# Gate and up of a SwiGLU feed-forward with the weights held in the array: 80 of 88 blocks computed transposed, in a two-layer-type transformer on one core

## The reference

```python
D_MODEL, SEQ, D_FF = 1024, 256, 2816

def rms_norm(x, g):
    y = x * lax.rsqrt(jnp.mean(x * x, axis=-1, keepdims=True) + 1e-6)
    return y * g

def swiglu(x, w_gate, w_up, w_down):
    return (jax.nn.silu(x @ w_gate) * (x @ w_up)) @ w_down

h = h + 0.5 * swiglu(rms_norm(h, g), w_gate, w_up, w_down)   # eight times, mixers between them
```

## Time and profile before

| | |
|---|---|
| median of 3 runs | 1973.38 us |
| lowest, highest | 1972.54, 1973.45 us |
| profiled execution, first to last instruction (the only time that it has) | 1971.0 us |
| PE, PEld busy | 1960.5, 1652.8 us |
| DVE, ACT, POOL busy | 1199.4, 1018.6, 68.9 us |
| TensorE clock granted | 1.000 |
| share of PE in the chain that ended last | 95% |

### The profile page before, as it was taken

The page is one execution under the profiler, slowest core; times in us unless marked ns, Lnnn a source line. Parts: engine busy times, 40 slices in busy tenths (PEclk is TensorE's granted clock), DMA queues, the critical chain, the costliest instruction groups (busy, mean ns, idle before and its releaser), DMA issues.

```text
span 1971.0 us, 26229 instructions
## 1 busy us (share of the span) xinstructions
PE 1960.5 (99%) x9838; PEld 1652.8 (84%) x9838; DVE 1199.4 (61%) x1817; ACT 1018.6 (52%) x1590; POOL 68.9 (3%) x77
## 2 busy tenths in 40 slices
PE   9999999999999999999999999999999999999999
PEld 7888988888888898888888898888888888888887
DVE  6555656556655566555755566655576555876554
ACT  6444555445554665444544447544475444755442
POOL 0100300000000000000000000000010000200000
PEclk9999999999999999999999999999999999999999
DMA  9655436553655426555555434555446553306550
GB/s 339 210 202 174 150 108 214 192 191 130 221 184 178 144 77 212 192 192 171 188 181 186 162 138 139 203 192 192 171 163 234 183 189 128 108 24 212 192 192 22
DMA packets 241050, 338.91 MB, mean 172 GB/s; under 512 B 5728, under 2 KB 206351, under 8 KB 240831
## 3 DMA queue, kind: packets, MB, share of 16 engines
q1 hardware_dynamic: 239710, 335.84, 50.5%
q0 software_dynamic: 496, 1.23, 0.2%
q10 hardware_dynamic: 752, 0.61, 0.1%
HBM read 336.61 MB, written 1.05 MB: 171 GB/s over the span
## 4 chain that ended last, share of the span: by engine, by line
PE 95%; DVE 2%; ACT 2%; DMA 1%; issue 0%; SPq 0%; POOL 0%; ACTq 0%
PE A L535 11%; PE A L537 11%; PE A L536 11%; PE G L535 10%; PE G L537 10%; PE G L536 10%; PE X L535 8%; PE X L537 8%; PE X L536 8%; PE A L1226 1%; PE A L904 1%; PE G L964 1%; PE X L964 1%; PE X L1210 1%; PE G L1238 1%; DVE wl L496 0%
## 5 line engine op out<-in xcount | busy, mean ns | idle before, releaser
L496 DVE TENSOR_TENSOR wl<-raw,wh 128x1024 fp32r<-128x1024 f32 (+1 forms) x553 | 653.8, 1221 | 121.3 <-ACT wh L487 120.3
L487 ACT ACTIVATE wh<-raw 128x1024 fp32r<-128x1024 f32 (+1 forms) x553 | 561.9, 1058 | 144.1 <-PE A L537 102.6
L535 PE MATMUL G<-wh,xh 128*128 128x512 f32 (+1 forms) x814 | 322.1, 396 | 0.2
L537 PE MATMUL G<-wh,xl 128*128 128x512 f32 (+1 forms) x814 | 317.2, 390 | 0.0
L536 PE MATMUL G<-wl,xh 128*128 128x512 f32 (+1 forms) x814 | 316.3, 389 | 0.0
L535 PE MATMUL X<-wh,xh 128*128 128x512 f32 x672 | 265.8, 395 | 0.3 <-DVE wl L496 0.3
L537 PE MATMUL X<-wh,xl 128*128 128x512 f32 x672 | 262.3, 390 | 0.0
L536 PE MATMUL X<-wl,xh 128*128 128x512 f32 x672 | 261.6, 389 | 0.0
L537 PEld LDWEIGHTS G<-wh,xl 128*128 128x128 f32 x814 | 152.8, 188 | 32.3
L535 PEld LDWEIGHTS G<-wh,xh 128*128 128x128 f32 x814 | 152.9, 188 | 30.9 <-DVE xl L2399 0.6
L536 PEld LDWEIGHTS G<-wl,xh 128*128 128x128 f32 x814 | 153.1, 188 | 29.9
(11 more groups left out here) (487 smaller groups left out, 2787.5 us busy)
## 6 DMA issues: line engine op xcount, KB each, us to landing
raw<-in_ffn_w_in SPq DMA_DIRECT2D x88, 1024.0 KB, 6.8
raw<-in_ffn_w_down SPq DMA_DIRECT2D x44, 1024.0 KB, 6.5
raw<-in_ffn_w_out SPq DMA_DIRECT2D x44, 1024.0 KB, 7.1
raw<-in_ffn_w_gate SPq DMA_DIRECT2D x42, 1024.0 KB, 5.5
raw<-in_ffn_w_up SPq DMA_DIRECT2D x42, 1024.0 KB, 7.5
raw<-in_a_w_in SPq DMA_DIRECT2D x12, 1024.0 KB, 6.1
raw<-in_ab_w_in SPq DMA_DIRECT2D x8, 1024.0 KB, 6.8
raw<-in_kv_w SPq DMA_DIRECT2D x6, 1024.0 KB, 6.5
```

Source lines behind the costliest of these rows:

```text
L487: nc.scalar.activation(hi, r, ACT.Copy).then_inc(hi_done[u], 1)
L496: nc.vector.tensor_tensor(lo, r, hi.bitcast(F32), ALU.subtract).then_inc(lo_done[u], 1)
L535: nc.tensor.matmul(o, sh, rh, start=start, stop=False)
L537: return nc.tensor.matmul(o, sl, rh, start=False, stop=stop)
```

## The change

In blocks 1 to 10 of every feed-forward the weights of gate and of up are stationary, 128 hidden columns at a time, and the tokens move. `xh` and `xl` are put side by side in one buffer `xs`, so one matmul of 512 columns gives high weights by high tokens (first half of the bank) and high weights by low tokens (second half). Eight of these and eight matmuls of 256 columns (low weights by high tokens, into the first half) make one bank: 128 hidden columns of gate or of up. A half of a block is now 128 hidden columns with all 8 chunks of channels. The hidden block comes out with hidden columns on partitions, so it isn't transposed.

The two halves of a bank are added by ACT (`lows`, copies the second half to SBUF) and DVE (`sums`). The factor of a token now runs along the free axis. DVE multiplies gate by `tok_rstd` (`normed`), ACT takes Silu (`gate`), DVE multiplies by up (`hidden`), ACT and DVE split (`hid_hi`, `hid_lo`). The factor of up is left to the residual add, which multiplies by `half_rstd` in place of 0.5. Block 0 stays as it was in its matmuls and is transposed, into banks A, with Silu in place of Sigmoid. Each feed-forward makes `tok_rstd` once by `turn_factor` with a matrix of ones. In ffn0 the loads of block 1 are cut by columns (512 bytes in a row in place of 1024).

The diff, cut to its core:

```diff
-        xh = sb("xh", [P, KC, S], F32R)
-        xl = sb("xl", [P, KC, S], F32R)
+        xs = sb("xs", [P, 2, KC, S], F32R)
+        xh, xl = xs[:, 0, :, :], xs[:, 1, :, :]
...
+            if spec == "ffn" and u < 2 and block not in first_ffn_blocks:
+                mode, shape = "cols", (KC, P)
+            elif spec == "ffn":
...
                     for u, w in ((0, gate), (1, up)):
-                        load_rows(sp, w, 1, u, slice(0, 4), raw_landed[1][u])
+                        load_cols(w, 1, u, 0, raw_landed[1][u])
...
                     tile = base + 2 * b + half
+                    if b > 1:
+                        pe.wait_ge(sums_done, 20 * f + 2 * (b - 2) + half + 1 + at)
+                    for u in (0, 1):
+                        pe.wait_ge(lo_done[u], n_of[tile, u] + at)
+                        _, sh, sl = half_views(tile, u)
+                        bank = GB[1 - half][u]
+                        for c in range(KC):
+                            mm(bank[:, :].rearrange("p (a s) -> p a s", a=2), sh[:, c, :], xs[:, :, c, :], start=c == 0,
+                               stop=False)
+                        for c in range(KC):
+                            last = mm(bank[:, 0:S], sl[:, c, :], xh[:, c, :], start=False, stop=c == KC - 1)
+                    last.then_inc(used[1], 1)
...
                 def step(b, turn=None):
                     gate_up(b, 0, turn)
-                    turn_hid(b - 1, turn)
+                    if b == 1:
+                        turn_first_hid()
+                        turn_factor(name, tok_rstd_in, ones)
                     gate_up(b, 1, turn)
                     down(b - 1, turn)
...
                 gate_up(end, 0)
-                turn_hid(end - 1)
                 gate_up(end, 1)
                 wait_down(end - 1)
...
-                    if q == 3:
-                        turn_hid(end)
...
-            def turn_factor(k):
+            def turn_factor(name, src, every):
-                pe.wait_ge(event("factor_in"), k)
+                pe.wait_ge(event("factor_in"), FACTOR[name])
                 for t in range(NT):
-                    last = mm(A[2][:, t * P:(t + 1) * P], tri[:, P:S], factor_in[:, t, :], start=True, stop=True)
+                    last = mm(A[2][:, t * P:(t + 1) * P], every, src[:, t, :], start=True, stop=True)
...
+                def lows(b, half, turn=None):
                     at = 0 if turn is None else 4 * turn
+                    by, n = done_at[base + 2 * b + half, 1]
                     act.wait_ge(used[by], n + at)
-                        A_(sig[:, t, :], GB[b % 2][t][:, 0:S], ACT.Sigmoid, scale=rstd[:, t:t + 1]).then_inc(sig_ready, 1)
+                    for u, dst in ((0, gate_n), (1, up_n)):
+                        last = A_(dst[:, half, :], GB[1 - half][u][:, S:2 * S], ACT.Copy)
+                    last.then_inc(low_out, 1)
...
+                def step(b, turn=None):
+                    for half in (0, 1):
+                        for u in (0, 1):
+                            prepare_hi(base + 2 * b + half, u, turn)
+                        lows(b - 1, half, turn)
+                    gate(b - 1, 0, 2, turn)
                     for half in (0, 1):
                         prepare_hi(base + 2 * b + half, 2, turn)
-                    hid_hi(b - 1, turn)
+                    hid_hi(b - 1, 0, 2, turn)
...
+                end = FFN_BLOCKS - 1
+                lows(end, 0)
                 prep(name, FT, (0, 1))
-                sigmoid(FFN_BLOCKS - 1)
+                gate(end, 0, 1)
+                hid_hi(end, 0, 1)
+                lows(end, 1)
+                gate(end, 1, 1)
...
+                def sums(b, half, turn=None):
                     at = 0 if turn is None else 4 * turn
+                    dve.wait_ge(low_out, 20 * f + 2 * (b - 1) + half + 1 + at)
+                    for u, dst in ((0, gate_n), (1, up_n)):
+                        last = V.tensor_tensor(dst[:, half, :], GB[1 - half][u][:, 0:S], dst[:, half, :], ALU.add)
+                    last.then_inc(sums_done, 1)
...
+                def step(b, turn=None):
+                    for half in (0, 1):
+                        for u in (0, 1):
+                            prepare_lo(base + 2 * b + half, u, turn)
+                        sums(b - 1, half, turn)
+                    normed(b - 1, 0, 2, turn)
+                    prepare_lo(base + 2 * b, 2, turn)
+                    hidden(b - 1, 0, 2, turn)
+                    prepare_lo(base + 2 * b + 1, 2, turn)
+                    hid_lo(b - 1, 0, 2, turn)
```

More of the change, by code:

```diff
@@ L931, in gate_up @@
                                 pe.wait_ge(lo_done[u], PIECE_AT[tile][i])
-                        if b == 0 and (tile or i):
+                        if tile or i:
                             if half == 0 and i == 2:
@@ L1787, in ffn, with first_gate, first_hid_hi @@
                 f, base = int(name[3:]), T0[name]
-                def sigmoid(b, turn=None):
+                def first_gate():
+                    by, n = done_at[base + 1, 1]
+                    act.wait_ge(used[by], n)
+                    for t in range(NT):
+                        A_(silu[:, t, :], GB[0][t][:, 0:S], ACT.Silu, scale=rstd[:, t:t + 1]).then_inc(silu_ready, 1)
+                def first_hid_hi():
+                    for t in range(NT):
+                        act.wait_ge(hid_turned, 2 * f + t + 1)
+                        A_(hidh[:, 0, t * S:(t + 1) * S], A[t][:, 0:S], ACT.Copy).then_inc(hidh_done, 1)
@@ L1797, in hid_hi, with gate @@
+                def gate(b, first, n, turn=None):
                     at = 0 if turn is None else 4 * turn
[L1798 to L1802, removed]
+                    act.wait_ge(gate_ready, 20 * f + 2 * (b - 1) + first + n + at)
+                    A_(silu[:, first:first + n, :], gate_n[:, first:first + n, :], ACT.Silu).then_inc(silu_ready, n)
@@ L1935, in fox_mixer @@
                 start("fox")
-                factor_out(1)
+                factor_out("fox")
                 def split_keys(b):
@@ L2457, in hid_lo, with first_hidden @@
-                def hid_lo(b, turn=None):
-                    at = 0 if turn is None else 4 * turn
-                    for t in range(NT):
-                        dve.wait_ge(hidh_done, 2 * (FFN_BLOCKS * f + b) + t + 1 + at)
-                        part = slice(t * S, (t + 1) * S)
-                        V.tensor_tensor(hidl[:, b % 2, part], GB[b % 2][t][:, 0:S], hidh[:, b % 2, part].bitcast(F32),
-                                        ALU.subtract).then_inc(hidl_done, 1)
-                def step(b, turn=None, split=(), downs=()):
+                def first_hidden():
+                    for t in range(NT):
+                        dve.wait_ge(silu_ready, 2 * FFN_BLOCKS * f + t + 1)
+                        V.tensor_tensor(hid[:, t, :], GB[0][t][:, S:2 * S], silu[:, t, :], ALU.mult).then_inc(hid_done, 1)
@@ new lines, in first_hid_lo @@
+                def first_hid_lo():
+                    for t in range(NT):
+                        dve.wait_ge(hidh_done, 2 * FFN_BLOCKS * f + t + 1)
+                        part = slice(t * S, (t + 1) * S)
+                        V.tensor_tensor(hidl[:, 0, part], A[t][:, 0:S], hidh[:, 0, part].bitcast(F32), ALU.subtract
+                                        ).then_inc(hidl_done, 1)
+                def sums(b, half, turn=None):
+                    at = 0 if turn is None else 4 * turn
+                    dve.wait_ge(low_out, 20 * f + 2 * (b - 1) + half + 1 + at)
+                    for u, dst in ((0, gate_n), (1, up_n)):
+                        last = V.tensor_tensor(dst[:, half, :], GB[1 - half][u][:, 0:S], dst[:, half, :], ALU.add)
+                    last.then_inc(sums_done, 1)
@@ new lines, in normed, with hidden @@
+                def normed(b, first, n, turn=None):
+                    at = 0 if turn is None else 4 * turn
+                    dve.wait_ge(sums_done, 20 * f + 2 * (b - 1) + first + n + at)
+                    part = gate_n[:, first:first + n, :]
+                    V.tensor_tensor(part, part, wide(tok_rstd.unsqueeze(1), n, S), ALU.mult).then_inc(gate_ready, n)
+                def hidden(b, first, n, turn=None):
+                    at = 0 if turn is None else 4 * turn
+                    dve.wait_ge(silu_ready, 2 * (FFN_BLOCKS * f + b) + first + n + at)
+                    part = slice(first, first + n)
+                    V.tensor_tensor(hid[:, part, :], up_n[:, part, :], silu[:, part, :], ALU.mult).then_inc(hid_done, n)
@@ L2466, in step, with hid_lo, first_step @@
+                def hid_lo(b, first, n, turn=None):
+                    at = 0 if turn is None else 4 * turn
+                    dve.wait_ge(hidh_done, 2 * (FFN_BLOCKS * f + b) + first + n + at)
+                    to, hi = (x[:, b % 2, S * first:S * (first + n)].rearrange("p (j s) -> p j s", s=S) for x in (hidl, hidh))
```

(2 more changed lines are left out.)

153 lines of the change are left out of this document (85 added, 68 removed).

## The result

The changed kernel takes 1959.13 us (median of four runs, 1959.00 to 1959.45) against 1973.04 us for the kernel before in the same comparison (1972.54 to 1973.45). The ratio is 0.9931, with a 95% interval of 0.9919 to 0.9943. The prediction was 1958.8 us, in a range of 1955 to 1966: 14.6 us less than the 1973.38 of the three runs before it, where 13.9 were measured.

What follows compares the result with a forecast made beforehand. PE was taken to bound the kernel, busy 1960.5 of 1971.0 us. 1971.0 - 18.3 (blocks) + 3.7 (factor) = 1956.4 us, with 2.4 us from span to median 1958.8 us; range 1955 to 1966 us.

Steps and rivals of the forecast that it cites:

- Transposes: PE, blocks 1 to 10: four transposes removed at 0.443 us a block, -35.4 us; 0.05 a block left as a rest.
- Gate and up: PE, blocks 1 to 10: 16 more matmuls a block cost +0.213 us each block, +17.1 us in all.
- changing between the widths costs nothing: PE, gate and up: going between matmuls of 512 and 256 columns adds no time, 0.
- The factor: PE, once per feed-forward: two matmuls of 128 columns, 0.46 us each time, +3.7 us; wait taken as 0.
- the wait of ffn4: PE at ffn4's first transposes: a 0.26 us wait for a weight tile on DVE, which the factor fills.
- The chain in a block: ACT and DVE work up to hidl: 14.0 us end to end against PE's 16.5, cover at least 2.5 us, no cost.
- (b): End of each feed-forward: chain late, seven hand-overs at 0.3 us each, 8 x 1.2 = +10, 1968 us; chance 0.12.
- the old order had the transposes there and more cover: End of a feed-forward: more cover before the change; now a 3.99 us chain leaves 1.45 us; cost taken as 0.
- (a): Matmuls of 256 in each block: weight load not hidden, 0.07 us each, +179 us, 2138 us; chance 0.04.
- (c): Start of ffn0: late by DMA and table load, +2 to +3 us, 1961 us; chance 0.06.
- (d): Gate and up: the 16 extra matmuls of a block cost nothing, 17.1 us stay away, 1942 us; chance 0.03.
- (e): Each block: new waits on sums_done or hidl_done, 80 x 0.3 us or more, 1978 to 1990 us; chance 0.03.

Runs made afterwards that it cites:

- e4: Changed kernel with four transposes of the identity put back between the half blocks of blocks 2 to 10, into a bank cleared afterwards: 1991.08 us.
- e1: Changed kernel with 28 of the 32 matmuls of 512 columns per block (gate and up, blocks 1 to 10) each cut into two of 256: 1985.68 us.
- e6: Changed kernel with the two matmuls that make the factor of the tokens run three times in each feed-forward: 1967.65 us.
- e7: Changed kernel with DVE's product of the last 128 hidden columns repeated three times more at the end of each feed-forward: 1961.97 us.
- e8: Changed kernel with DVE's product of the last 128 hidden columns repeated six times more at the end of each feed-forward: 1972.10 us.
- e2: Changed kernel with the 16 wide matmuls of gate and up first in each half block and the 16 narrow ones behind them: 1956.29 us.
- e3: Changed kernel with wide and narrow matmuls alternating by chunk of channels, 32 changes from narrow to wide per block: 1973.36 us.

## Why the prediction was right

**The mechanism.** PE's issue time is the time, and the change moves it by what its matmuls and transposes cost. That held: -13.9 us, where the sum was -18.3 + 3.7 = -14.6. No engine took PE's place.

**Transposes, -35.4 us forecast.** e4 gives 0.444 us for a block where 0.443 was taken. But of the 0.49 us that a block lost over its 72 matmuls, I left 0.05 in the block as a rest. It went too: in the trace before, the wide matmuls that follow are slow by 0.05 us together until they are back at 0.2267, so it was a cost of the transposes.

**Gate and up, +17.1 us forecast.** The 16 instructions more cost 0.213 us a block by the cadences, and e1 confirms the price of 13 ns for each from another side. The step that was mis-sized is "changing between the widths costs nothing". I had read it from wide to narrow, the direction that is free. From narrow to wide it is not, and the block has four of these: 16.61 - 32 x 0.2267 - 32 x 0.120 - 24 x 0.2267 = 0.08 us. The two slips nearly cancel, 0.05 against 0.08, and the block came out 0.03 us longer than forecast: -16.0 us in 80 blocks in place of -18.3.

**The factor, +3.7 us forecast.** 0.111 us for each of four pieces, 3.6 us by e6. No wait came with it. In the changed kernel the wait of ffn4 is gone, as said.

**The other 1.3 us.** 80 blocks at -0.20 us and the factor make -12.4, and 13.7 were measured from block 1 on. The two traces laid side by side show where the rest is. Between the feed-forwards it is only 0.3 us. A feed-forward that no wait disturbs (ffn5, ffn6) gains 1.61 us, 0.05 more than ten blocks and the factor give, 0.4 in all. The kernel before lost 0.3 us at the end of ffn2 and 0.5 at the start of ffn4, of which the earlier trace rows show 0.26 as idle time; both losses are gone. The changed kernel loses 0.2 at the end of ffn0 (e7). The end of ffn2 in the kernel before, where `down(end)` starts 0.47 us behind the matmul before it and not 0.23:

```profile
656.00 0.40 PE L537 MATMUL A<-mh,hidl 128*128 128x512 f32 x1
656.47 0.47 PE L535 MATMUL A<-wh,hidh 128*128 128x512 f32 x1
```

**What was luck.** The forecast is 0.3 us off by a sum of slips: +2.3 for the blocks, -1.3 for the rest above, -0.1 for the factor, and -0.6 because I took a run to last 2.4 us longer than its span, from two different executions, where it is 1.8 (1959.17 to 1957.4 in the profiled one). That the terms are right within 2 to 3 us isn't luck; that the total is right within 0.3 is.

**Covers.** The chain in a block was counted at 14.0 us put end to end, with 2.5 of cover. In the trace `hidl` is done 6 us ahead of `down`. At the end of a feed-forward the count was 3.99 us, without hand-overs, and 3.94 were seen from the start of `down(end - 1)` with the hand-overs in it. The hand-overs between ACT and DVE are short, where rival (b) put each at 0.3 us, for which it had no row:

```profile
1104.63 0.42 ACT L1845 ACTIVATE hidh<-work 128x256 fp32r<-128x256 f32 x1 [0.49 <-DVE work L2543]
```

This copy ends at 1105.05 and `hidl` starts at 1105.08, 0.03 us later. The cover was put at 1.45 us less the hand-overs; about 1.4 of it are there. What was wrong is "the old order had the transposes there and more cover". It had less. DVE and PE at the end of ffn4 in the kernel before:

```profile
1114.49 0.76 DVE L2462 TENSOR_TENSOR hidl<-G,hidh 128x256 fp32r<-128x256 f32 x2 [0.37 <-ACT hidh L1800]
```
```profile
1115.49 0.40 PE L535 MATMUL A<-wh,hidh 128*128 128x512 f32 x1
```

`hidl` was ready at 1115.25, 0.24 us ahead of `down(end)`, and so at seven ends. In e8, where PE waits for it, 0.15 us lie between the two, so 0.1 us was free; at the end of ffn2 it was too late. It waits 0.37 us for `hidh`, and `hidh` for PE's transposes, which stood ahead of the last quarter of `down(end - 1)` alone. Without them the chain starts at the end of `gate_up(end, 1)`, and the end of a feed-forward has become safer.

**The rivals.** (a) fell by e1. (b), the late end, would have cost about what e8 shows had the chain been 2.7 us longer; it is real, and about 1.4 us away. (c): PE starts block 1 at 20.62 us, 0.22 us behind the last matmul of block 0, and block 0's transposes at 26.18, 0.12 us behind a narrow matmul, so it waits neither for the rows of 512 bytes nor for the table. (d) fell by e1: extra matmuls do cost 13 ns. (e): no wait on `sums_done` or `hidl_done` in any block.

## What to carry to other kernels

Where TensorE is busy all the time, compare two tilings by the distances between matmul starts: columns over the clock and a fixed price per matmul with its load (here 13 ns, at 256 and at 512 columns), whatever the durations in the profile say. Take the price from rows of the same kind: the float32 pieces of 128 columns start every 0.11 us here and don't follow it. Keeping weights stationary gives an output that needs no transpose for the next product, and its price is the number of matmuls, since a moving side of 256 tokens fills only half of one. Put narrow matmuls together in one run, and count what the chain at the end of a stage has for cover, as it is the shortest there (1.5 us here, against 6 inside).

## What the runs showed of the hardware

The weight loads of e1's narrow matmuls (group by form: count, busy us, mean ns, idle before):

```profile
L945 PEld LDWEIGHTS G<-xs,wh 128*128 128x128 f32 x2240 | 290.5, 190 | 7.8
```

A weight load lasts 0.19 us, and 22 matmuls of 256 columns in each bank, each with a load of its own, still start every 0.120 us (e1). Matmuls of 512 columns are slow by 0.02 to 0.03 us together behind a run of narrow ones, and this is no wait (e2). Behind four transposes it is 0.05 us (the kernel before). The loss of a block is 0.08 us with four changes and 0.26 with 32 (e3), not eight times as much. A piece of a transpose is shown with 0.27 us and starts every 0.11; four cost 0.44 us (e4) to 0.49 (the kernel before) with the slowness behind them. From the end of an instruction on ACT to the start of the one on DVE that waits for it are 0.03 us at the end of a feed-forward.
